# An encoder layer's MLP: the seven products of the second matrix product in another order, summed in PSUM

## What is computed

```python
x = x + mix @ w_out
h = _rmsnorm(x, mlp_norm_w) @ w_mlp1          # 1024 -> 4096
x = x + jnp.square(jax.nn.relu(h)) @ w_mlp2   # 4096 -> 1024
gate = jax.nn.sigmoid(x @ w_ple_gate)
x = x + gate * _rmsnorm(p_l @ w_ple_proj, ple_norm_w)
```

## Time and profile before

| | |
|---|---|
| median of 3 runs | 1787.55 us (1785.61 to 1788.14) |
| span of the profiled execution | 1784.8 us |
| TensorE busy | 1742.3 us, 98% |
| TensorE weight loads | 1581.7 us, 89% |
| VectorE busy | 1328.8 us, 74% |
| ScalarE busy | 728.7 us, 41% |
| GpSimd busy | 406.7 us, 23% |
| chain that ended last, by engine | TensorE 83%, VectorE 10%, ScalarE 3%, DMA 2% |
| products 112 to 223 | 1225.77 to 1632.57 us of the span |

### The profile page before, as it was taken

How to read it: one execution, slowest core, us unless ns; L and a number is a source line. 1 busy time by engine, 2 the same in 40 slices (tenths; PEclk the granted TensorE clock), 3 DMA queues, 4 the chain that set the end, 5 groups by cost and what they waited for, 6 DMA issues and landing times.

```text
span 1784.8 us, 26437 instructions
## 1 busy us (share of the span) xinstructions
PE 1742.3 (98%) x10563; PEld 1581.7 (89%) x10563; DVE 1328.8 (74%) x1671; ACT 728.7 (41%) x1149; POOL 406.7 (23%) x256
## 2 busy tenths in 40 slices
PE   8999999999999999999999999999899999999999
PEld 5576788888899987888999999999899999998887
DVE  4696486887999988579765555557999898996634
ACT  6112221157777787146333333334333333334511
POOL 0000000003222220002222221225848373740000
PEclk9999999999999999999999999999999999999999
DMA  9223155141100013423232222329241414002121
GB/s 362 88 95 121 57 177 188 48 160 68 64 30 21 16 74 108 143 107 139 90 126 88 100 99 88 107 77 342 81 157 45 166 34 149 35 1 77 36 95 59
DMA packets 59058, 183.65 MB, mean 103 GB/s; under 512 B 6901, under 2 KB 7669, under 8 KB 58424
## 3 DMA queue, kind: packets, MB, share of 16 engines
q1 hardware_dynamic: 58936, 181.96, 28.7%
HBM read 138.58 MB, written 43.35 MB: 102 GB/s over the span
## 4 chain that ended last, share of the span: by engine, by line
PE 83%; DVE 10%; ACT 3%; DMA 2%; issue 2%; SPq 1%; POOL 0%; DVEq 0%; ACTq 0%; POOLq 0%
PE ps L3247 40%; PE ps L2724 23%; PE ps L3107 3%; PE ps L3135 3%; PE ps L3119 2%; PE ps L2783 2%; PE ps L2810 2%; PE ps L2822 1%; DVE ptl L2299 1%; DVE gmax L2252 1%; PE ps L3016 1%; PE ps L2771 1%; PE ps L3028 1%; DMA wst<-wb 1%; DVE ringl L2463 1%
## 5 line engine op out<-in xcount | busy, mean ns | idle before, releaser
L3247 PE MATMUL ps<-rV,ringh 128*128 128x320 f32 x1248 | 235.9, 311 | 8.7 <-issue 6.8
L3247 PE MATMUL ps<-rU,ringh 128*128 128x320 f32 x1088 | 204.3, 310 | 2.6 <-issue 1.4
L3247 PEld LDWEIGHTS ps<-rV,ringh 128*128 128x128 f32 x1248 | 197.3, 189 | 10.4 <-issue 8.0
L2724 PE MATMUL ps<-XL,wh 128*128 128x512 f32 x708 | 178.1, 360 | 0.0
L3247 PEld LDWEIGHTS ps<-rU,ringh 128*128 128x128 f32 x1088 | 170.5, 188 | 4.1 <-issue 2.7
L2480 DVE TENSOR_TENSOR fH<-ps,fH 128x640 f32<-128x640 f32 x112 | 90.8, 823 | 111.8 <-PE ps L3247 111.7
L2724 PE MATMUL ps<-XH,wh 128*128 128x512 f32 (+1 forms) x612 | 164.3, 377 | 6.1 <-DVE wl L1632 2.8
L2724 PE MATMUL ps<-XH,wl 128*128 128x512 f32 (+1 forms) x612 | 153.9, 360 | 0.0
L3247 PE MATMUL ps<-rV,ringl 128*128 128x320 f32 x624 | 143.0, 310 | 0.0
L2724 PEld LDWEIGHTS ps<-XH,wh 128*128 128x128 f32 x612 | 104.7, 191 | 39.5 <-issue 18.3
L3247 PE MATMUL ps<-rH,ringh 128*128 128x320 f32 x736 | 137.8, 309 | 1.3 <-DVE rH L2425 1.3
(11 more groups left out here) (408 smaller groups left out, 3886.3 us busy)
## 6 DMA issues: line engine op xcount, KB each, us to landing
hd<-fH SPq DMA_DIRECT2D x64, 320.0 KB, 2.3
wst<-wb SPq DMA_DIRECT2D x34, 512.0 KB, 3.7
wst<-wm SPq DMA_DIRECT2D x30, 512.0 KB, 3.7
fU<-hd SPq DMA_DIRECT2D x32, 320.0 KB, 3.9
fH<-hd SPq DMA_DIRECT2D x24, 320.0 KB, 3.9
wraw<-wm SPq DMA_DIRECT2D x14, 512.0 KB, 3.7
w2b<-wm SPq DMA_DIRECT2D x12, 512.0 KB, 6.9
xraw<-xT SPq DMA_DIRECT2D x8, 640.0 KB, 10.0
```

The lines of the kernel that those rows point to most:

```text
L2724: ins = mm(acc(jslot)[:, o:o + n], sub(a[slot], s), b[:, o:o + n], start=(first and k == 0 and a is wh and b is xh), stop=(last and k == l ...
L3247: ins = mm(out[:, c, :], a[:, w], two(b(xs[kk]))[:, c, :], start=kk == 0 and a is h and b is hi_of, stop=kk == 3 and a is l)
```

## The change

The seven kinds come in another order (a new index g for them): (b,0) x a12, (a,0) x a11, T2 x S2, T1 x S1, (b,1) x S4, T3 x S3, T4 x a22. The products of g = 2, 3 and 4 don't clear their PSUM slot: they add to what g = 1 and their forerunners left there, and g = 6 adds to g = 5. VectorE adds each of the 28 results of a block to exactly one quarter of X, while the slot keeps its content for the next product. The helper tile and its copies and sums are gone; its place holds T1 instead, which is now computed out of place. GpSimd's operations keep their number (32 in a block) and stand in another order; SyncE reloads the hidden kinds 3, 2, 1, 0 of the next block in this order, and weights `w2a` before `w2b`. SyncE's order for block 0 is not changed but for the last three groups of X.

```diff
-        first_sum = [("V1", 0), ("V1", 1), ("V4", 0), ("V4", 1)]
+        t1_at = [("V1", 0), ("V1", 1), ("V4", 0), ("V4", 1)]
...
+        def second_source(g, kk):
+
+            a, b = hid[kk]
+            return [raw(b, 0), raw(a, 0), raw(a, 0), raw(*t1_at[kk]), raw(b, 1), raw(a, 1), raw(a, 0)][g]
+
+        def second_weight(i):
+
+            g, p = (i - 112) % 28 // 4, i % 4
+            f1, f2 = w2a[p], w2b[p]
+            return [f1[:, BANK:1024], f1[:, 0:BANK], w2tmp[p % 2], f2[:, 0:BANK], f1[:, BANK:1024], f1[:, 0:BANK],
+                    f2[:, BANK:1024]][g]
...
-            for g in (2, 3, 1):
+            for g in (3, 2, 1):
                 load_sum(g)
             for c in range(1, 4):
-                for kind, q in ((1, 3), (2, 4), (0, 5), (3, 6)):
-                    sp.wait_ge(n_lo, operand_lo_done(4 * (7 * (c - 1) + q) + 3))
+                sp.wait_ge(n_lo, operand_lo_done(4 * (7 * (c - 1) + 4) + 3))
+                load_hidden(c, 3)
+                sp.wait_ge(t_add, second_added(c - 1, T4, 3))
+                load_hidden(c, 2)
+                for kind, g in ((1, 5), (0, 6)):
+                    sp.wait_ge(n_lo, operand_lo_done(4 * (7 * (c - 1) + g) + 3))
                     load_hidden(c, kind)
                 for p in range(4):
                     sp.wait_ge(w_lo, weight_lo(112 + 28 * (c - 1) + 20 + p))
-                    load_w2(c, p, True)
+                    load_w2(c, p, False)
                 for p in range(4):
                     sp.wait_ge(w_lo, weight_lo(112 + 28 * (c - 1) + 24 + p))
-                    load_w2(c, p, False)
-            sp.wait_ge(w_lo, weight_lo(112 + 84 + 23))
+                    load_w2(c, p, True)
...
-                if q in (0, 1, 6):
-                    kind = {0: 0, 1: 2, 6: 3}[q]
-                    act.wait_ge(h_in[kind], H_IN + 64 * (c + 1))
+                if g in (0, 1, 4):
+                    act.wait_ge(h_in[{0: 2, 1: 0, 4: 3}[g]], H_IN + 64 * (c + 1))
                 else:
-                    act.wait_ge(t_add, second_added(c, {3: 0, 2: 1, 4: 2, 5: 3}[q], kk))
-                src = [raw(a, 0), raw(b, 0), raw(a, 0), raw(a, 1), raw(b, 0), raw(a, 0), raw(b, 1)][q]
-                fn(hi_of(buf[j % 3][kk]), src, ACT.Copy).then_inc(n_hi, 1)
+                    act.wait_ge(t_add, second_added(c, {2: T2, 3: T1, 5: T3, 6: T4}[g], kk))
+                fn(hi_of(buf[j % 3][kk]), second_source(g, kk), ACT.Copy).then_inc(n_hi, 1)
...
-            def second_add(c, kind, kk):
+            def second_add(c, name, kk):
 
                 a, b = hid[kk]
-                if kind == 0:
+                if name == T3:
                     pool.wait_ge(h_in[1], H_IN + 64 * (c + 1))
                     pool.wait_ge(h_in[3], H_IN + 64 * (c + 1))
                     G.tensor_tensor(raw(a, 1), raw(b, 1), raw(a, 1), ALU.subtract).then_inc(t_add, 1)
-                elif kind == 1:
-                    pool.wait_ge(n_lo, operand_lo_done(28 * c + kk))
-                    pool.wait_ge(t_add, second_added(c, 0, kk))
+                elif name == T2:
+                    pool.wait_ge(n_lo, operand_lo_done(28 * c + 4 + kk))
+                    pool.wait_ge(t_add, second_added(c, T3, kk))
                     G.tensor_tensor(raw(a, 0), raw(a, 1), raw(a, 0), ALU.add).then_inc(t_add, 1)
-                elif kind == 2:
-                    pool.wait_ge(n_lo, operand_lo_done(28 * c + 4 + kk))
-                    pool.wait_ge(t_add, second_added(c, 1, kk))
-                    G.tensor_tensor(raw(b, 0), raw(b, 0), raw(a, 0), ALU.subtract).then_inc(t_add, 1)
+                elif name == T1:
+                    if c == 0:
+                        pool.wait_ge(mm_done, product_done(111))
+                    pool.wait_ge(t_add, second_added(c, T2, kk))
+                    G.tensor_tensor(raw(*t1_at[kk]), raw(b, 1), raw(a, 0), ALU.subtract).then_inc(t_add, 1)
                 else:
                     pool.wait_ge(n_lo, operand_lo_done(28 * c + 8 + kk))
-                    G.tensor_tensor(raw(a, 0), raw(b, 1), raw(a, 0), ALU.subtract).then_inc(t_add, 1)
-
-            def second_weights(c, kind, p):
+                    pool.wait_ge(h_in[2], H_IN + 64 * (c + 1))
+                    pool.wait_ge(t_add, second_added(c, T1, kk))
+                    G.tensor_tensor(raw(a, 0), raw(b, 0), raw(a, 0), ALU.subtract).then_inc(t_add, 1)
...
             for c in range(4):
                 for kk in range(4):
-                    second_add(c, 0, kk)
+                    second_add(c, T3, kk)
                 for kk in range(4):
-                    second_add(c, 1, kk)
+                    second_add(c, T2, kk)
+                    second_add(c, T1, kk)
+                for p in range(0, 4, 2):
+                    for k in range(2):
+                        second_weights(c, "S3", p + k)
+                        second_weights(c, "S2", p + k)
+                    for k in range(2):
+                        second_weights(c, "S4", p + k)
                 for p in range(4):
-                    second_weights(c, 3, p)
-                for p in range(2):
-                    second_weights(c, 2, p)
-                    second_weights(c, 4, p)
-                for kk in range(2):
-                    second_add(c, 2, kk)
-                for p in range(2, 4):
-                    second_weights(c, 2, p)
-                    second_weights(c, 4, p)
-                for kk in range(2, 4):
-                    second_add(c, 2, kk)
-                for p in range(4):
-                    second_weights(c, 1, p)
+                    second_weights(c, "S1", p)
                 for kk in range(4):
-                    second_add(c, 3, kk)
+                    second_add(c, T4, kk)
...
             def output_sum(i):
 
-                c, q, p = i // 28, i % 28 // 4, i % 4
-                base = PS_READ + 112
+                c, g, p = i // 28, i % 28 // 4, i % 4
                 dve.wait_ge(mm_done, product_done(112 + i))
                 x11, x12 = tok(X, p)[:, 0:HALF], tok(X, p)[:, HALF:T]
                 x21, x22 = tok(X, 4 + p)[:, 0:HALF], tok(X, 4 + p)[:, HALF:T]
-                s16 = raw(*first_sum[p])
                 if i >= 4:
-                    dve.wait_ge(ps_read, base + i - 3)
-                if c == 0 and i == 0:
-                    dve.wait_ge(n_lo, operand_lo_done(0))
-                if c == 0 and q in (1, 3, 5):
-                    for g in {1: (0,), 3: (2, 3), 5: (1,)}[q]:
-                        dve.wait_ge(x_in[g], 48 + 64 + (16 if g == MORD[6] else 0))
-
-                def add(x):
-
-                    return V.tensor_tensor(two(x), two(x), slot(112 + i), ALU.add)
-
-                if q == 0:
-                    if c:
-                        add(s16)
-                    else:
-                        V.tensor_copy(two(s16), slot(112 + i)).then_inc(ps_read, 1)
-                        return
-                    add(x11).then_inc(ps_read, 1)
-                elif q == 3:
-                    add(x22)
-                    add(x21).then_inc(ps_read, 1)
-                elif q == 5:
-                    add(x22)
-                    add(x12).then_inc(ps_read, 1)
-                else:
-                    add({1: x11, 2: s16, 4: x21, 6: x12}[q]).then_inc(ps_read, 1)
-                if c == 3 and q in (2, 4, 5) or c == 0 and q == 1:
-                    dve.wait_ge(ps_read, base + i + 1)
-                    x = {1: x11, 2: x12, 4: x21, 5: x22}[q]
-                    st.link(V.tensor_tensor(x, x, s16, ALU.add))
+                    dve.wait_ge(ps_read, PS_READ + 112 + i - 3)
+                if c == 0 and g in (0, 2, 3, 4):
+                    q = {0: 0, 2: 3, 3: 2, 4: 1}[g]
+                    dve.wait_ge(x_in[q], 48 + 64 + (16 if q == MORD[6] else 0))
+                x = [x11, x11, x21, x22, x12, x22, x21][g]
+                V.tensor_tensor(two(x), two(x), slot(112 + i), ALU.add).then_inc(ps_read, 1)
...
-            def product(i, xs, waits=()):
+            def product(i, xs, waits=(), fresh=True):
 
                 pe.wait_ge(w_lo, weight_lo(i))
                 h, l = ring[i % 4]
@@ -3245,7 +3224,7 @@
                     for a, b in ((h, hi_of), (h, lo_of), (l, hi_of)):
                         for c in range(2):
                             ins = mm(out[:, c, :], a[:, w], two(b(xs[kk]))[:, c, :],
-                                     start=kk == 0 and a is h and b is hi_of, stop=kk == 3 and a is l)
+                                     start=fresh and kk == 0 and a is h and b is hi_of, stop=kk == 3 and a is l, skip_group_check=not fresh)
...
-                product(112 + i, buf[j % 3], [(n_lo, operand_lo_done(4 * j + kk)) for kk in range(4)])
+                product(112 + i, buf[j % 3], [(n_lo, operand_lo_done(4 * j + kk)) for kk in range(4)], j % 7 in (0, 1, 5))
```

(34 more changed lines are left out.)

24 lines of the change are left out of this document (8 added, 16 removed).

## The result

The changed kernel takes 1790.2 us (median of 20 runs, 1787.3 to 1792.8), the kernel before 1788.0 (20 runs, 1785.3 to 1789.5): ratio 1.0017 [1.0011, 1.0023]. That is 2 to 4 us slower where 4.45 were forecast (1792 against 1787.55): slower, clear of zero by the interval, by a little less than the 0.2% that was taken as what a measurement can tell from no change, and inside the range. The profiled execution spans 1790.0 us, against 1784.8.

What follows compares the result with a forecast made beforehand. TensorE, busy 98%, bounds the kernel, with losses only in the first 14 of the last 112 products. From 1784.8: +7.3 at product 120, -4.8 old loss, +2.1 clock gives 1789.4; plus 2.75 to the median, 1792 us, range 1786 to 1797.

Steps and rivals of the forecast that it cites:

- the two waits: Block 0's start: ScalarE waits for hidden kind 2, then VectorE for X's first four loads, landing at 1247.3.
- first rounding for 112: ScalarE rounds product 112's first operand tile at 1222.2, 4.1 us later, since hidden kind 2 lands at 1222.0.
- idle inside 112: TensorE idles 2.6 and 1.2 us inside product 112, low parts of its operand tiles coming late on VectorE.
- last relu ends: VectorE finishes product 111's result and relu at 1236.7 instead of 1231.85, 4.85 us lost.
- first add into X: VectorE's add of product 112's result waits for X's first four loads, the last landing at 1247.3.
- first result to 119's low weights: VectorE's line from product 112's result to product 119's low weights takes 10.3 us, against 11.1 before.
- from there to 120's low weights: VectorE's five low parts, a result and weights take 10.95 us, to 1268.65, against 12.2 before.
- half clock after 120, cost: TensorE idle before products 116 and 120 brings half clock costing 1.7 to 2.5 us, possibly nought at the short gap.
- 120 to 126: Old loss of 4.8 us goes, leaving only half clock; product 126 starts at 1291.6 to 1292.4.
- the part, against before: From product 112 to the next stage: +7.3 at product 120, -4.8 old loss, +2.1 clock, in all +4.6 us.
- rival (b): Block 0: both waits are covered and saved VectorE work wins, 5.2 us faster, 1782.4 us; chance 0.10.
- The likeliest case: Whole kernel: forecast of 1792 us with its spread, 1790 to 1795; chance 0.50.

Runs made afterwards that it cites:

- 84 more adds: Changed kernel with 28 more adds from PSUM into X in each of blocks 1 to 3: 1795.69 us, ratio 1.0044 to the kernel before.
- 36 more adds: Changed kernel with 12 more adds from PSUM into X in each of blocks 1 to 3: 1790.66 us, ratio 1.0018 to the kernel before.
- X earlier: Changed kernel with X's first four loads issued ahead of the last stores of hidden tiles: 1785.98 us, ratio 0.9991 to the kernel before.
- waits put into the kernel before: Kernel before plus two waits alone, ScalarE's for hidden kind 2 and VectorE's for X's first four loads: 1793.88 us, ratio 1.0030.
- kind 2 earlier: Changed kernel with block 0's hidden kind 2 loaded ahead of kind 1 on SyncE: 1786.41 us, ratio 0.9993 to the kernel before.
- both: Changed kernel with hidden kind 2 and X's first four loads both moved earlier on SyncE: 1784.05 us, ratio 0.9978 to the kernel before.
- Its columns taken away: Changed kernel with both SyncE moves, 24 of GpSimd's 32 block 0 operations cut to 8 columns: 1772.30 us, ratio 0.9916 to the kernel before.
- a step later: Changed kernel with both SyncE moves, operand tiles from the fourth kind on handled one step later: 1783.26 us, ratio 0.9977 to the kernel before.
- onto VectorE: Changed kernel with both SyncE moves, block 0's T2 and T1 sums on VectorE, later operand tiles delayed two steps: 1782.88 us, ratio 0.9980.
- held back: Kernel with T2 and T1 sums on VectorE, GpSimd also waiting in block 0 for product 120's low weights: 1782.23 us, ratio 0.9969.

## Why the prediction was right, and where it was off

Right: the place (products 112 to 126), the two waits, the order in which they act, and that the VectorE work saved in blocks 1 to 3 is worth nothing. Step by step, measured times first as they stand in the execution of after, which runs 0.77 us late at product 112:

| step | predicted | measured |
|---|---|---|
| first rounding for 112 | 1222.2 | 1222.53 |
| idle inside 112 | 2.6 + 1.2 | 0.77 + 0.95 |
| last relu ends | 1236.7 | 1237.1 |
| first add into X | 1247.3 | 1247.38 |
| first result to 119's low weights | 10.3 | 8.7 |
| from there to 120's low weights | 10.95 | 11.2 |
| product 120 starts | 1268.75 | 1267.45 |
| half clock after 120, cost | 1.7 to 2.5 | 1.6 |
| 120 to 126 | 22.8 to 23.6 | 23.07 |
| the part, against before | +4.6 | +2.9 |

**The term that was mis-sized** is VectorE's line from the first result to product 120, "result 0.75, weights 0.6, low parts 0.75 and 2.15", 10.3 us in the sum and 8.7 in the trace. Timeline of VectorE and GpSimd:

```profile
1248.72 0.82 DVE L2525 TENSOR_TENSOR rU<-fV,rU 128x640 fp32r<-128x640 f32 x1
...
1254.84 1.32 DVE L2470 TENSOR_TENSOR ringl<-w2a,ringh 128x512 fp32r<-128x512 f32 x1
...
1249.61 2.06 POOL L1578 TENSOR_TENSOR fV<-fV 128x640 f32<-128x640 f32 x1 [2.68 <-DVE rU L2525]
```

I priced the second low part at 2.15 us as though a GpSimd add stood beside it. In fact GpSimd had done what it could in the 6.75 us for which VectorE waited for X, and was itself waiting for VectorE's low part (the 2.68 us in the last line); both low parts took 0.82. So 1.6 us of the X wait came back. Counted from product 112, X also arrived 0.7 us sooner than forecast, and product 120 is 5.2 us behind before's, not 7.3.

**The idle inside product 112 is not one number.** The weights' low part was priced behind GpSimd's first add. In after it ran at 1226.37 in 0.69 us, 0.35 ahead of that add (1226.72). But in the run with 84 more adds, whose code is the same up to block 1, the order was the forecast's. Its timeline of GpSimd, VectorE and TensorE:

```profile
1227.21 2.18 POOL L1574 TENSOR_TENSOR fU<-fH,fU 128x640 f32<-128x640 f32 x1 [34.42 <-DMA fU<-hd]
1227.90 2.04 DVE L2470 TENSOR_TENSOR ringl<-wraw,ringh 128x512 fp32r<-128x512 f32 x1
1232.07 0.85 PE L3229 MATMUL ps<-rH,ringh 128*128 128x320 f32 x4 [3.80 <-DVE rH L2525]
```

The idle was 3.80 and 0.95 us, and the first add into X came 22.9 us after product 112's start, against 20.8 in after and 20.5 in the run with 36 more adds. So one and the same code gives about 2 us more or less here, by which of the two engines comes first by a few tenths of a microsecond; after's trace is one draw. The runs with X earlier and with the waits put into the kernel before show the long idle as well (3.19 and 3.61 us).

**Where the wait for X hides a cost.** The same length, first result to product 120, is 20.1 us in after, in the run with kind 2 earlier and in both runs with more adds, which all wait for X, and 23.8 in the two runs of this order that don't (X earlier, both). While VectorE waits, GpSimd gets ahead and out of its way; without the wait they run side by side. So 3.7 us of any gain at X's arrival is given back, and rival (b), which took 21.25 us (10.3 + 10.95) for a stage without the wait, was too kind: from its first result at 1238.03 it had product 120 at 1259.3, and the run has it at 1260.39 from a first result at 1236.59. Whether the two waits' costs add up can't be told: taken away singly they give 0.24 and 0.26%, together 0.39%, with intervals of 0.09% on each.

**Not foreseen:** gaps of 0.18 and 0.34 us before 126 and 127 (0.9 us lost in all), where the prediction had TensorE free of idle from 1292.

**The size, and where it was luck.** The likeliest case said slower by over 0.2%, with a sum of 0.25%; the runs say 0.17%, 0.11 to 0.23. The mis-sized term is 1.6 us, 0.09%, about the difference. The forecast of 1792 stands on two further things that the sum can't claim. In every run on record the time lies 1.73 to 1.84 us above the span of its core, not 2.75; the rest of that term was that the profiled execution of before had been about 1 us quicker than the median of its three runs. And the two profiled spans lie 5.2 us apart, near the forecast's 4.6, only because the tail of after fell 1.5 us longer and its product 112 0.77 later; the part itself grew by 2.9.

**The clock.** Granted clock in windows after product 120 starts, the first of after (idle 1.94 us before it), the second of the run with kind 2 earlier (2.43 us):

```profile
1267.45:1272.00 4.55, 4.55 (x21) 4.55 (x22) 4.55 (x4) 0.00 (x0) 4.41 (x4) 0.62 0.01 4
...
1264.60:1268.00 3.40, 3.40 (x23) 3.40 (x24) 3.40 (x4) 0.00 (x0) 3.26 (x3) 1.00 0.00 0
```

In after the engine runs at 1.2 GHz for most of 4.55 us; in the other, behind a longer idle, at 2.4 throughout. The Trainium skill (TensorE: Matmul & The Clock Gate, Part 1) says that the chip's watch runs free of the kernel; by that rule the outcome at such a gap is a matter of where it falls, and the traces agree: 1.94 us of idle cost 1.6 us of clock, 2.43, 2.79 and two of 2.45 cost none. The clearest case is the idle of 2.05 us before the next stage, the same in eleven of the twelve traces: half clock followed in seven of them and not in four. Idle of 4.2 us and more was followed by half clock each time, at 1.4 to 2.6 us. The prediction said that its clock term could be nought at a short gap, but summed up with 1.7 to 2.5; for idle of 1.9 to 2.8 us the term is nought to 1.6 in these traces, and 1.4 to 2.6 from 4.2 us on; before a product none lies between.

## What to carry to other kernels

Work taken off an engine with slack counts only in the stage where that engine is late; before counting it, list what the new order needs first in that stage and when its load was issued, since here two waits, on loads whose place in the queue nobody moved, cost more than 60 removed instructions gave. A wait of one of two engines that slow each other is partly paid back, since the other gets ahead meanwhile; price what follows such a wait as if the two did not slow each other, and what follows its removal as if they did. And after such a change try the queue order at once: here two moved groups of loads turn 0.17% slower into 0.22% faster.

## What the runs showed of the hardware

**Adds from PSUM don't slow beside GpSimd.** VectorE's lines in blocks 1 to 3 of the run with 84 more adds (busy us, mean ns, idle before):

```profile
L2543 DVE TENSOR_TENSOR X<-X,ps 128x640 f32<-128x640 f32 x99 | 80.1, 809 | 7.0 <-PE ps L3229 7.0
L2542 DVE TENSOR_TENSOR X<-X,ps 128x640 f32<-128x640 f32 x83 | 67.2, 809 | 6.6 <-PE ps L3229 6.6
...
L2525 DVE TENSOR_TENSOR rU<-fH,rU 128x640 fp32r<-128x640 f32 x8 | 12.8, 1605 | 0.0
```

An add with one operand in PSUM takes 809 ns on average with GpSimd busy half of the time; in this group a low part of the same size with both operands in SBUF takes 1605. Sorted by what GpSimd does meanwhile, in the same trace from 1300 to 1640 us: 58 of the adds lie wholly beside a GpSimd instruction and take 808 ns, 102 meet none and take 810; 15 low parts lie wholly beside one and take 2024 ns, 46 meet none and take 813. The Trainium skill (SBUF — State Buffer, Who interferes with whom) has this as a rule, that a VectorE instruction with at most one SBUF input does not contend with GpSimd; the trace agrees.

**How much of this stage is GpSimd's.** Its columns taken away were worth 11.1 us, nearly three times the gain from the 60 removed instructions, and none of the ways to move that work (a step later, onto VectorE, held back) brought more than 2 by the ratios: in the first and the last of them what VectorE didn't lose beside GpSimd came back as waits for late sums. What share is contention and what share lateness stays open; a run that takes one away and leaves the other was not made.
